# Two-block transformer, feed-forward: one silu behind a copy, the up piece queued first, three accumulators, terms spread anew

## The reference, cut to what matters

```python
for layer in range(2):
    ...                                            # four mixers, w_out, residual
    h = rmsnorm(x, norm_ffn[layer])
    x = x + (silu(h @ w_gate[layer]) * (h @ w_up[layer])) @ w_down[layer]
return rmsnorm(x, norm_final)
```

```python
c_act = silu(c)
for i in range(2):
    mods = c_act @ ada_w[i] + ada_b[i]             # 1024 x 6144, a vector of 6 x 1024
    sh_m, sc_m, g_m, sh_f, sc_f, g_f = split(mods, 6)
    ...                                            # a convolution, then a mixture of 32 experts
```

## Time and profile before

| | before |
|---|---|
| runs, us | 2069.62, 2069.80, 2076.03; median 2069.8 |
| the profiled execution, us | 2073.47 |
| its span, us | 2071.7 |
| PE busy | 1898.6 us, 92% |
| DVE busy | 863.3 us, 42% |
| ACT busy | 332.1 us, 16% |
| chain that ended last | PE 62%, DMA 24%, DVE 7% |
| mean granted TensorE clock | 0.97 |

### The profile page before, as it was taken

The page is one execution under the profiler, slowest core; times in us unless marked ns, Lnnn a source line. Parts: engine busy times, 40 slices in busy tenths (PEclk is TensorE's granted clock), DMA queues, the critical chain, the costliest instruction groups (busy, mean ns, idle before and its releaser), DMA issues.

```text
span 2071.7 us, 21123 instructions
## 1 busy us (share of the span) xinstructions
PE 1898.6 (92%) x8030; PEld 965.4 (47%) x8030; DVE 863.3 (42%) x1560; ACT 332.1 (16%) x783; POOL 87.1 (4%) x129
## 2 busy tenths in 40 slices
PE   8988999999889999899999999998998999889886
PEld 4555555445555654765434343333775333323321
DVE  1466688834767888765111111112325011111113
ACT  2442111024421111222100010000102000000000
POOL 3102000001020000300000000000000000000000
PEclk9999999999999999999999999999999999999999
DMA  9215767562157677555999999999355999999995
GB/s 309 83 57 163 256 251 279 212 227 62 57 193 288 230 264 264 189 183 191 374 414 428 426 428 428 427 428 407 113 192 214 384 430 428 427 429 427 428 426 232
DMA packets 149241, 603.12 MB, mean 291 GB/s; under 512 B 16584, under 2 KB 60536, under 8 KB 121232
## 3 DMA queue, kind: packets, MB, share of 16 engines
q1 hardware_dynamic: 144064, 591.43, 72.6%
q0 software_dynamic: 4880, 10.22, 1.8%
q10 hardware_dynamic: 192, 0.05, 0.0%
HBM read 597.67 MB, written 1.10 MB: 289 GB/s over the span
## 4 chain that ended last, share of the span: by engine, by line
PE 62%; DMA 24%; DVE 7%; DVEq 2%; issue 2%; ACT 1%; ACTq 1%; SPq 1%
PE ps L2487 14%; DMA ring<-in_e_w_gate 13%; PE ps L907 10%; DMA ring<-in_e_w_up 8%; PE ps L635 7%; PE ps L990 6%; PE ps L2319 4%; PE ps L2505 4%; PE ps L2251 3%; PE ps L2332 3%; PE ps L731 2%; PE ps L2431 2%; PE ps L2416 1%; DMA ring<-in_e_w_down 1%; DMA ring<-in_w_up 1%
## 5 line engine op out<-in xcount | busy, mean ns | idle before, releaser
L2487 PE MATMUL ps<-ring,hT 128*64 128x512 f32 (+1 forms) x1056 | 240.4, 607 | 33.6 <-DMA ring<-in_e_w_up 17.2
L2505 PE MATMUL ps<-ring,qkT 128*64 128x512 f32 (+1 forms) x1024 | 226.6, 594 | 9.9 <-ACT qkT L2707 7.9
L2487 PE MATMUL ps<-ring,late 128*32 128x512 f32 (+1 forms) x928 | 211.1, 609 | 24.0 <-DMA ring<-in_e_w_up 12.7
L635 PE MATMUL ps<-ring,hT 128*128 128x512 f32 (+1 forms) x384 | 169.3, 592 | 3.0 <-DMA ring<-in_w_in 2.2
L2487 PEld LDWEIGHTS ps<-ring,hT 128*64 128x64 f32 (+1 forms) x1056 | 77.3, 126 | 193.1 <-issue 193.1
L2976 DVE TENSOR_TENSOR qkT<-ps,qkT 128x512 f32<-128x512 f32 (+1 forms) x64 | 44.2, 690 | 255.6 <-PE ps L2505 255.6
L2999 DVE TENSOR_TENSOR qkT<-ps,qkT 128x512 f32<-128x512 f32 (+1 forms) x32 | 22.1, 690 | 297.8 <-PE ps L2487 297.8
L2487 PEld LDWEIGHTS ps<-ring,late 128*32 128x32 f32 (+1 forms) x928 | 68.6, 125 | 161.9 <-issue 161.9
L2505 PEld LDWEIGHTS ps<-ring,qkT 128*64 128x64 f32 (+1 forms) x1024 | 70.9, 123 | 146.2 <-issue 146.2
L1612 DVE SCALAR_TENSOR_TENSOR qkT<-ring,cc,qkT 128x512 f32<-128x512 f32 x168 | 125.9, 749 | 8.5
L635 PEld LDWEIGHTS ps<-ring,hT 128*128 128x128 f32 x384 | 72.3, 195 | 80.0 <-issue 70.3
(11 more groups left out here) (433 smaller groups left out, 2238.8 us busy)
## 6 DMA issues: line engine op xcount, KB each, us to landing
ring<-in_e_w_down SPq DMA_DIRECT2D x64, 2048.0 KB, 17.0
ring<-in_e_w_up SPq DMA_DIRECT2D x64, 2048.0 KB, 17.3
ring<-in_e_w_gate SPq DMA_DIRECT2D x60, 2048.0 KB, 17.5
ring<-in_ada_w SPq DMA_DIRECT2D x24, 2048.0 KB, 14.2
ring<-in_w_gate SPq DMA_DIRECT2D x16, 1408.0 KB, 8.7
ring<-in_w_up SPq DMA_DIRECT2D x16, 1408.0 KB, 9.3
ring<-in_w_down SPq DMA_DIRECT2D x22, 1024.0 KB, 5.1
ring<-in_w_in SPq DMA_DIRECT2D x8, 2048.0 KB, 11.6
```

What stands on the lines that cost most here:

```text
L635: last = mm(m.ps[:, 4 + i, 0:chunk_width(n)], m.hT[:, j, i * P:(i + 1) * P], w[:, j, :], start=(j == 0), stop=(j == KC - 1))
L2487: last = mm(dst, xg[:, j, at + x * n_tok:at + x * n_tok + place], w(x, j), start=(j == 0), stop=(j == KC - 1))
L2505: lasts[x] = mm(dst, m.hidT[:, j, rows + x * place:rows + (x + 1) * place], half_of(w(x, j), n), start=(j == 0), stop=(j == 3))
```

## The change

Four edits, all in the feed-forward and its modulation work:

- ScalarE: silu21 of step k-1 stands behind the copy of P6(k) in odd steps, in the list TAKEN and in the code.
- SP: up_load(1) is issued ahead of matrix 1.
- Three accumulators instead of two (N_ACC); the third takes 512 columns behind the first two. The first term of matrix k waits for the sum of matrix k - 3 instead of k - 2. TensorE's wait before it sums matrix k in the up stage now asks for k rows made (rows 0 to k - 1), where it asked for k - 1, and in layer 0 it applies from k = 1 instead of k = 2.
- ADA_TERMS: step 7 has 7 terms instead of 9, step 8 has 2 instead of 3, steps 9 to 17 have 3 each, where steps 8 to 16 had.

```diff
@@ TAKEN
-        TAKEN += [("silu22", _k - 1), ("silu12", _k - 1), ("silu21", _k - 1)]
+        TAKEN += [("silu22", _k - 1), ("silu12", _k - 1)]
     TAKEN.append(("P6", _k))
+    if _k % 2 == 1:
+        TAKEN.append(("silu21", _k - 1))
@@
+N_ACC = 3
-ADA_TERMS = [6] + [9] * (N_FU - 1) + [3] * 9 + [0] * (N_DC - 9)
+ADA_TERMS = [6] + [9] * 6 + [7] + [2] + [3] * 9 + [0] * (N_DC - 10)
@@ place
-    m.ada_acc = q[:, 7168:8192].rearrange("p (b n) -> p b n", b=2)
+    m.ada_acc = q[:, 7168:8704].rearrange("p (b n) -> p b n", b=N_ACC)
@@ first_sync
         up_load(0)
         ada(0)
+        up_load(1)
         ada(1)
-        up_load(1)
         ada(2)
@@ first_tensor, ada_sums
                 if n < N_FU:
-                    if L > 0 or k >= 2:
-                        ready("ada_row", k - 1)
+                    if L > 0 or k >= 1:
+                        ready("ada_row", k)
...
-                    last = mm(dst[32 * g:32 * (g + 1), :], m.ones[:, 0:32], m.ada_acc[:, k % 2, g * P:(g + 1) * P], start=True, stop=True)
+                    last = mm(dst[32 * g:32 * (g + 1), :], m.ones[:, 0:32], m.ada_acc[:, k % N_ACC, g * P:(g + 1) * P], start=True, stop=True)
@@ first_scalar
                 gated(k - 1, 1, 1)
                 gated(k - 1, 0, 1)
+            kept(k, "P6")
+            if k % 2 == 1:
                 gated(k - 1, 1, 0)
-            kept(k, "P6")
@@ first_vector, ada_term
-                if L > 0 or k >= 2:
-                    dve.wait_ge(s["ada_ps"], nth(L, "ada_ps", k - 1))
+                if L > 0 or k >= N_ACC:
+                    dve.wait_ge(s["ada_ps"], nth(L, "ada_ps", k - N_ACC + 1))
...
-            acc = m.ada_acc[:, k % 2, :]
+            acc = m.ada_acc[:, k % N_ACC, :]
```

## The result

The changed kernel takes 2081.65 us (median of six runs, 2078.50 to 2085.84); the kernel before, in the same comparison, 2071.02 (six runs). The ratio is 1.0048, 95% interval 1.0030 to 1.0066: slower by about 10 us, where +9.4 was forecast. A second comparison later gave 1.0055 (1.0038 to 1.0072). The profiled execution took 2078.50 us with a span of 2076.7; it was the fastest of its six, while that of before (2073.47) lay above its median.

A forecast was written before the change was run, and what follows sets the result against it. TensorE, busy 92% of the span, was taken as the bound, so its gaps were priced: -6.0 - 4.0 + 8.4 + 2.7 + 8.3 = +9.4, giving 2079.2 us on the median 2069.8; range 2073 to 2086, forecast's chance 0.60.

The forecast's parts named there:

- Part 1: Layer 0's up stage: loading the up piece ahead of matrix 1 removes a 3.06 us wait and slow products; 6.0 gained.
- The gate piece: Layer 0, up step 2: this weight load becomes late next, losing 0 to 3.3 us; 0.5 taken.
- Part 2: Up stages, step 3: silu move and three accumulators gain 2.0 us a layer, 4.0 in all, despite a new wait.
- The new wait: Step 3 of both up stages: TensorE's sums of matrix 2 wait 4.1 us for VectorE's row 1.
- Part 3, layer 0: Layer 0's end: last sums behind the last product delay VectorE's tail, 8.4 us lost, plus 2.7 for the clock.
- T: End of a layer's last product; forecast at 424.17 in layer 0 and 830.49 in layer 1.
- Part 3, layer 1: Layer 1's end: the same late tail delays the second block's first product; 8.3 us lost.
- (a): The clock does not fall in step 3's new hole; 5.5 us less for two layers, 2073.7; chance 0.14.
- (b): Row 1 comes in time, or nearly, in step 3; 13.8 us less, 2065.4; chance 0.08.
- (c): The next layer's first product waits for a weight load anyway, covering the tail; 2059.8; chance 0.06.
- (d): Step 2's gate piece over 2 us late (+5), or clock costs 2 more at layer ends; 2082 to 2086; chance 0.12.
- The small edits at nothing: Fewer terms in step 7, matrix 8 summed two down steps later, and later projection loads; priced at nothing.

The follow-up runs named there:

- before's second profile: The kernel before, unaltered, run and profiled again: 2071.34 us, ratio 1.0008.
- later sums: The changed kernel with the old ADA_TERMS list and matrices 2 to 6 summed one step later: 2062.35 us, ratio 0.9950 to the kernel before.
- the old terms: The changed kernel with the ADA_TERMS list of the kernel before: 2065.12 us, ratio 0.9964 to the kernel before.
- the accumulators alone: The kernel before with three accumulators and TensorE's wait for row k, silu21 in its old place: 2066.37 us, ratio 0.9975.
- the terms alone: The kernel before with only the new ADA_TERMS list: 2091.15 us, ratio 1.0097.
- filled: The changed kernel with 14 unused matmuls behind each layer's last sums: 2087.29 us in a single execution.
- one a step: The changed kernel with the old ADA_TERMS list and matrices 2 to 8 summed one step later: 2052.53 us, ratio 0.9904 to the kernel before.

## Why the prediction was right, point by point

**The total.** Forecast +9.4; measured +10.6 between the medians, about +9.9 and +11.4 by the two ratios. The forecast case came, by its own terms: the waits that it named are in the trace. Its sizes were less good than its total. With the sizes found below the sum is -3.7 - 5.8 + 10.7 + 8.1 = +9.3; the first two were off by 2.3 and 1.8 in opposite directions, and that they cancelled is luck.

**Part 1, -6.0.** Right in the first profile (6.5 with the clock), but -3.7 in the runs (95%: -6.0 to -1.7, so the miss itself is loose). The term that was mis-sized here: it was read from one wait of 3.06, and that wait is a matter of the run (1.57 to 3.82, and 2.46 in before's second profile). The bounds 6.5 and 0.5 held. The gate piece was in time (its product at 222.17 has no wait), so the 0.5 for it was not needed.

**Part 2, -4.0.** The new wait, its place, its releaser and its length (4.14 and 4.58 for 4.1) came as forecast. Mis-sized was the clock behind it: the sums and the next product took from 255.79 to 260.12, 4.33; in the kernel with later sums, which has no hole there, the same took 2.83 (254.22 to 257.05). That is 1.5, where 2.75 was in the sum. So layer 1 gained 2.6 and layer 0 9.7 - 6.5 = 3.2, where 2.0 each had been put. The hole's length doesn't set this price. In both profiles of the changed kernel and in that of the old terms, the holes of 4.15 and 4.6 cost 1.5 to 1.7 in either layer; with the accumulators alone, holes of the same length (4.15 and 4.59) cost 2.5 and 3.0, as the prediction had it. Why they do isn't shown, so a part of the 1.8 may be of the run.

**Part 3, layer 0: 8.4 + 2.7.** The tail at T + 1.9 and the last add done at 422.76 = T + 9.3 (forecast 9.2). Projection at T + 12.64, where before has 3.71: 8.9. Of these 8.9 the tail is 9.26 - 0.80 = 8.5, where 8.4 was put, and the way from the last add to the projection, 3.38 instead of 2.91, is 0.5, where 0.7 was put. The first transposes now start before the last adds and wait for VectorE in between, so their 5.20 to the projection, at a clock of 0.50, can't be set against the 3.21 of before. The projection itself took 22.42 instead of 20.68 (from the row of before's second profile), 1.7 where 2.0 was put; with the terms alone, behind the same wait of 7.08, it took 23.75. Sum 10.7, forecast 11.1.

**Part 3, layer 1: 8.3.** 846.57 is T + 16.69, before's T + 8.38: 8.3. Two errors cancel in it. The last add started at 840.25, T + 10.4 and not T + 8.6, as one group of three adds took 3.76 us instead of the 2.05 of layer 0 (the changed kernel's VectorE, and in the last line its POOL at that time):

```profile
833.76 3.76 DVE L1746 TENSOR_TENSOR x<-qkT,x 128x512 f32<-128x512 f32 x3
...
840.25 0.69 DVE L1746 TENSOR_TENSOR x<-ps,x 128x512 f32<-128x512 f32 x1
...
834.92 2.06 POOL L1965 TENSOR_TENSOR late<-fold,z 128x1024 f32<-128x1024 f32 x1 [228.72 <-DMA mods<-qkT]
```

and from there to the product it was 6.3 instead of 8.0. In the first profile of before an instruction behind the adds (L383, 832.80) took 1.87 us, 0.15 in its second profile, and layer 1's end was 1.7 shorter there. All fourteen profiles tell more. The group x<-qkT,x took 3.75 or 3.76 in the three (the changed kernel's two and the filled one) in which that POOL instruction started while the group ran, and 2.05 in the eleven in which it started when the group was over, or in its last 0.1 us. The adds that read PSUM (x<-ps,x) took 2.48 also with POOL beside them. The instruction at L383 started 0.37 us behind a POOL instruction in ten profiles and was slow in five of them; in the other four, where none had started before it, it was never slow. So VectorE is held up beside POOL, by 1.7 us, in some overlaps and not in others; what decides it at L383 stays open. That each of the two profiles compared had one such delay, and the 8.3 came out, is luck; without any, the terms alone against before's second profile give 97.5 - 89.4 = 8.1.

**A wrong sentence.** "That the clock is already low there costs nothing that the rows show" compared 32 instructions of 5.86 with a quarter of 128 instructions of 24.53; that row holds several shapes and names the first. The filled kernel has the same 32 at full clock: 3.81. The low clock costs 2.0 there in before (5.86), 1.4 in the changed kernel (5.20). It is paid in both, so the sum kept standing. The Trainium skill, "TensorE: Matmul & The Clock Gate", Part 1, says that an idle array falls to half its clock and that work then runs at half speed for a while; the prediction held against it, and the rows here side with the page.

**The rivals.** (a) fell: the product behind the hole took 3.75 instead of 2.37, but at about half the price put on it. (b) fell: row 1 came 4.14 late. (c) fell: nothing covered the tail. (d) didn't come. The small edits at nothing show none of their own: layer 0's up stage is 140.4 with the new terms and with the old. One of them was misread: by the two lists matrix 8 is summed one down step later, not two.

**What is left of the ledger.** It has +3.9 in the attention and -2.7 in the second block. Of the first, 1.7 is the projection's clock, which is in part 3, and 2.2 is before's first profile, since its second took 178.6. The second block varies by 8 us among kernels that don't differ in it.

## What to carry to other kernels

When a planner's list moves the last piece of side work by one step, look where that step stands: here it was the one behind the last product, and three terms of 96 put the whole tail of a layer behind it, 16.5 us for a list of numbers. A third buffer moves a wait to the next resource that two items share; spread the items so that no step holds two, and the waits go (2065.12 with pairs, 2052.53 with one a step). Profile the kernel before twice before a wait for a load is priced, for its length may be of that run.

## What the runs showed of the hardware

The same instruction sequence waited 1.57, 1.78, 2.46, 3.06 or 3.82 us for the same load. Behind the first two the product ran at full speed (2.47 us to the next, as at 209.83 above); behind 2.46 it took 4.0, and behind 3.82 it took 4.85 (its row and that of the 3.06 in the earlier trace rows both have 5.06). Waits of about the same length were not paid alike: behind the 4.14 of the changed kernel the product took 3.75, behind the 4.15 of the accumulators alone 4.78; behind the 4.58 in layer 1 of the changed kernel 3.80, behind the 4.58 of the earlier trace rows 4.85. A group of three VectorE adds with no operand in PSUM took 3.75 us in the three profiles in which a POOL instruction started while it ran, and 2.05 in the eleven others; four adds with one operand in PSUM took 2.48 with POOL beside them and without. Between kernels that differ by a few us elsewhere, the second block took 1230 to 1238 us, so that a gain of 4 us is seen in medians of ten runs and not in one profile.
